# The first pair of feed-forward column tiles turned by VectorE's 32x32 blocks and transfers, in place of TensorE transposes

## What is computed

```
D_MODEL = 1024
SEQ = 256
DEPTH = 2
FFN_HIDDEN = -(-8 * D_MODEL // (3 * 256)) * 256
...
        h = rms_norm(x, norm_ffn[l])
        gate, up = jnp.split(h @ ffn_in[l], 2, axis=-1)
        x = x + (jax.nn.silu(gate) * up) @ ffn_down[l]
```

## Time and profile before

| | |
|---|---|
| median of 3 runs | 904.03 us |
| the profiled execution | 905.12 us |
| its span in the trace | 903.1 us |
| TensorE busy | 893.1 us, 99% of the span |
| VectorE busy | 669.1 us, 74% |
| ScalarE busy | 513.9 us, 57% |
| TensorE's share of the chain that ended last | 93% |

### The profile page before, as it was taken

One profiled execution on the slowest core, in us unless ns is written; L12 is line 12 of the kernel. 1 busy time (PEld: TensorE's weight loads), 2 busy tenths in 40 slices (PEclk: granted clock), 3 DMA queues, 4 the chain that ended last, 5 costly groups with the idle time before them and its releaser, 6 DMA issues.

```text
span 903.1 us, 13837 instructions
## 1 busy us (share of the span) xinstructions
PE 893.1 (99%) x5410; PEld 761.2 (84%) x5410; DVE 669.1 (74%) x1107; ACT 513.9 (57%) x877; POOL 2.4 (0%) x6
## 2 busy tenths in 40 slices
PE   9999999999999999999999999999999999999997
PEld 5999898888887888888889998988888888888885
DVE  6869887778968666656778798767988675665656
ACT  6586556785446544444565866568744554444444
POOL 0000000000000000000000000000000000000000
PEclk9999999999999999999999999999999999999998
DMA  8645646657664777678655374486667467768671
GB/s 294 205 167 164 202 127 180 238 201 230 200 234 153 219 198 251 213 211 261 214 181 175 119 213 155 126 236 229 209 203 237 149 213 221 250 188 259 219 205 46
DMA packets 129056, 180.55 MB, mean 200 GB/s; under 512 B 82272, under 2 KB 88160, under 8 KB 128992
## 3 DMA queue, kind: packets, MB, share of 16 engines
q1 hardware_dynamic: 128560, 179.34, 62.8%
q10 hardware_dynamic: 432, 0.34, 0.1%
HBM read 169.16 MB, written 10.49 MB: 199 GB/s over the span
## 4 chain that ended last, share of the span: by engine, by line
PE 93%; DVE 5%; ACT 1%; issue 0%; ACTq 0%; DVEq 0%
PE bank L620 8%; PE bank L622 7%; PE bank L621 7%; PE bank L492 7%; PE bank L494 7%; PE bank L493 7%; PE bank L697 6%; PE bank L395 5%; PE bank L434 5%; PE bank L436 5%; PE bank L435 5%; PE bank L396 5%; PE bank L397 5%; PE bank L424 2%; PE bank L423 2%; PE bank L422 2%
## 5 line engine op out<-in xcount | busy, mean ns | idle before, releaser
L938 ACT CAST whi<-raw 128x1024 fp32r<-128x1024 f32 x290 | 303.6, 1053 | 296.3 <-PE bank L494 94.5
L1288 DVE TENSOR_TENSOR wlo<-raw,whi 128x1024 fp32r<-128x1024 f32 x290 | 347.6, 1216 | 66.7 <-ACT whi L938 64.1
L395 PE MATMUL bank<-ahi,whi 128*128 128x256 f32 x448 | 129.6, 289 | 0.8 <-DVE tmp L1338 0.8
L396 PE MATMUL bank<-alo,whi 128*128 128x256 f32 x448 | 126.7, 283 | 0.0
L397 PE MATMUL bank<-ahi,wlo 128*128 128x256 f32 x448 | 126.6, 283 | 0.0
L620 PE MATMUL bank<-whi,ahi 128*128 128x512 f32 x288 | 114.8, 399 | 0.6 <-DVE alo L1352 0.5
L622 PE MATMUL bank<-whi,alo 128*128 128x512 f32 x288 | 112.4, 390 | 0.0
L621 PE MATMUL bank<-wlo,ahi 128*128 128x512 f32 x288 | 112.3, 390 | 0.0
L492 PE MATMUL bank<-whi,ahi 128*128 128x512 f32 x288 | 112.2, 390 | 0.0
L494 PE MATMUL bank<-whi,alo 128*128 128x512 f32 x288 | 112.1, 389 | 0.0
L493 PE MATMUL bank<-wlo,ahi 128*128 128x512 f32 x288 | 112.0, 389 | 0.0
(11 more groups left out here) (299 smaller groups left out, 1305.8 us busy)
## 6 DMA issues: line engine op xcount, KB each, us to landing
raw<-stream_dram SPq DMA_DIRECT2D x292, 512.0 KB, 4.7
turned_dram<-proj SPq DMA_DIRECT2D x144, 32.0 KB, 1.7
proj<-turned_dram SPq DMA_DIRECT2D x18, 256.0 KB, 4.6
proj<-gbias_dram SPq DMA_DIRECT2D x12, 256.0 KB, 4.4
probs_dram<-proj SPq DMA_DIRECT2D x8, 192.0 KB, 4.3
proj<-probs_dram SPq DMA_DIRECT2D x2, 768.0 KB, 5.9
par<-params_dram SPq DMA_DIRECT2D x2, 556.5 KB, 6.5
x<-x_dram SPq DMA_DIRECT2D x2, 512.0 KB, 5.3
```

What stands on the lines that cost most here:

```text
L395: pe.matmul(dst, whi_of(m)[:, wcol], hi, start=first, stop=False, skip_group_check=True)
L396: pe.matmul(dst, whi_of(m)[:, wcol], lo, start=False, stop=False, skip_group_check=True)
L938: act.copy(whi_of(m), raw_of(m)).then_inc(*AC.up(("hi", m), "w"))
L1288: dv.tensor_tensor(wlo_of(m), raw_of(m), whi_of(m), ALU.subtract).then_inc(*DV.up(("lo", m), "w"))
```

## The change

Pair 0 takes the second way as well, in both layers. Its transfers stand at SP's f = 8 (writes) and f = 9 (read). `ffn_turned(0)` is 7 in place of 6; the down product stays at f = 8 and 9. The count by which ScalarE knows the returned transfers goes up accordingly. `turn_hidden` is no longer called.

```
         def ffn_turned(j):
 
-            return 6 * j + 6 if j < PAIRS - 1 else 6 * j + 3
+            return 6 * j + 6 if j else 7
...
         def by_transfer(j):
-            return 1 <= j < PAIRS - 1
+            return 0 <= j < PAIRS - 1
...
         def hid_count(l, j):
-            return l * (PAIRS - 2) + j
+            return l * (PAIRS - 1) + j + 1
...
                 for k in range(NH):
                     j, r = divmod(k - 2 * FFN0 - 6, 6)
+                    if k - 2 * FFN0 in (8, 9):
+                        j, r = 0, k - 2 * FFN0 - 8
+                    elif j == 0:
+                        r = None
                     if r == 0 and by_transfer(j):
```

## The result

The changed kernel takes 914.18 us (median of 6 runs, 911.87 to 917.14) against 904.46 (6 runs). The ratio is 1.0109, with a 95% interval of 1.0089 to 1.0128. It is slower by about 9.7 us; 911.6 was forecast, inside a range of 907.4 to 915.4.

What follows compares the result with a forecast made beforehand. TensorE was taken to bound the kernel. To the median of 904.03 us were added 5.6 for net stalls in two layers and 2.0 for one clock fall, giving 911.6 us, range 907.4 to 915.4.

Steps and rivals of the forecast that it cites:

- The bound: Whole kernel: TensorE, busy 99% of the span and 93% of the last chain, sets the time.
- The gain: Before f = 8: removing four transposes a layer saves 0.48 and 0.49 us, 0.97 us in two layers.
- The route: Pair 0's hidden values, from S (start of the first L1799) to the down product: 12.45 us, losing 2.8 a layer.
- The read at 303.90: S + 6.44: SP's queue, priced from pair 1: the read is issued 6.44 us after S, the start of the first L1799.
- the median of 4.6: Pair 0's read: lands 4.6 us after issue, the median of 18 reads ranging from 3.3 to 6.2.
- One fall in two stalls: TensorE's clock behind the stalls at f = 8: drops to half speed once, costing 2.0 us; chance 0.37.
- The two-fall rival: TensorE's clock falls behind both layers' stalls: 913.6 us, up to 915.6 with 3 us each; chance 0.17.
- the bound of 3 us: TensorE after a stall: 6 us of work at half speed lose 3 us, the upper bound for one fall.
- What was priced at nothing: VectorE's block transposes, SP's late loads 93 and 94, work queued behind ScalarE's and VectorE's waits: no cost.
- A quick read: Pair 0's read lands in 2.6 us, taking 2.0 off each layer's 2.8: 905.6 us; chance 0.05.
- A hidden read: Pair 0's read lands within 1.3 us of issue, so 0.97 us are won: 903.1 us; chance 0.04.
- Slower transfers: Writes collide with load 92 or an issue hangs in both layers: 913.0 us, 917 with two falls; chance 0.09.

Runs made afterwards that it cites:

- e8_tanh_first: Changed kernel with pair 0's down product at f = 10 and 11 and pair 1's tanh and hidden values ahead of pair 0's copy and remainder: 904.14 us, ratio 0.9997.
- e9_down12: Changed kernel with pair 0's down product at f = 12 and 13, its copy and remainder at f = 9: 903.53 us, ratio 0.9992.
- e2_load92: Changed kernel with the load of half 92 issued behind pair 0's read instead of before its writes: 914.67 us, ratio 1.0108.
- e3_loads92_93: Changed kernel with the loads of halves 92 and 93 both issued behind pair 0's read: 908.28 us, ratio 1.0045.
- e7_turned6: Changed kernel with pair 0's copy and remainder at f = 6 in place of 7: 914.30 us, ratio 1.0116.
- e1_fill: Changed kernel with unused matmuls filling TensorE's stalls before pair 0's down product, 16 in layer 0 and 10 in layer 1: 911.52 us, ratio 1.0087.
- e4_unused: Changed kernel with pair 0's transfers made but not waited for, TensorE's transposes used as in the kernel before: 904.42 us, ratio 0.9999.
- e5_later: Changed kernel with pair 0's down product two steps later, f = 10 and 11, copy and remainder at f = 8: 904.98 us, ratio 1.0006.

## Why the prediction was right

**The bound.** TensorE sets the end; every us that it stood or ran slowly is in the time: 9.7 by parts, 9.7 between the medians.

**The gain.** Two times 0.48 us were taken from the gap in the stream. The versions with the wait taken away come 0.1 (e8_tanh_first) and 0.7 us (e9_down12) under the kernel before by their medians, which proves nothing at this size. Their traces do: 0.49 us less from S to the end in layer 1, and 0.5 in layer 0, as priced.

**The route.** It was priced at 12.45 us from S. It took 13.65 in layer 0 and 11.94 in layer 1, 12.8 on average, so the two layers lost 4.0 and 2.3 us net in place of 2.8 each, 6.3 against 5.6. The total is near; the terms are not. "The read at 303.90: S + 6.44" was too small for pair 0 by 0.9 and 1.5 us: the collision with load 92, which the prediction left to the range, is real (e2_load92), and an issue hung in layer 0. The landing was quicker than the median of 4.6: 4.2 and 3.1 us. The last term, 1.41, was 1.5. That the errors nearly cancel is partly luck, and partly not: the late writes pushed the reads to 1.9 and 2.0 us behind the load before them, where the 18 stood at 1.2, and reads that far behind a load land sooner (see e3_loads92_93). The prediction took the median "since this read goes out behind a load just as the 18 do"; it did not.

**The clock.** This was the uncertain step. One fall in two stalls at 2.0 us was taken; two came, at 1.7 us each. So the branch that the forecast stood on, one fall (chance 0.37), is not what happened; the one with two falls (0.17) is, and the range held since it reached that far. One fall in two was halfway between two readings of the rows and was read from neither. The mis-sized term is their number, and it is the largest part of what is missing between 911.6 and 914.2. The two-fall rival named 913.6.

The rows for the clock were weak as well: the prediction had 1.9 us into idle time, from the end of the kernel before. In the six stalls that brought a fall (two each in the changed kernel, e2_load92 and e7_turned6) it came 3.2 to 5.1 us after the last matmul had ended, and at the ends of the other ten kernels 2.3 to 4.9 us after. The same holds for the bound of 3 us: the first short weight load stands 6.6 us after the first matmul in the kernel before, but 3.3 to 5.8 us after it in the other ten.

That a fall is what makes the matmuls slow, and that the standing makes the fall, is shown by e1_fill. How often it falls was not to be read from the trace before: stalls of 2.6 us (changed kernel, layer 1), 2.5 (e2_load92, layer 1) and 2.4 (e7_turned6, layer 1) brought a fall, one of 2.4 (e3_loads92_93, layer 0) did not. The Trainium skill, "TensorE: Matmul & The Clock Gate", section "HAM oscillation", says that each wait for a transfer between groups of matmuls can cost a fall, and half of the time spent low: by that rule the changed kernel's two stalls agree, 3.4 us low near each and 1.7 us lost. The two of e3_loads92_93, 2.4 and 1.6 us, brought no fall.

**What was priced at nothing.** The block transposes, the extra transfers, the late loads: e4_unused shows 0.9999. `ffn_turned(0)` = 7: e7_turned6 shows no effect. `hi(92)`, `lo(91)` and pair 1 behind the waiting instructions: no second wait in the changed kernel, as forecast; but only because TensorE had stood still as well. In e5_later, where it had not, just that queue became the next wait, in layer 0. The prediction's sentence "none is late next, as TensorE has stood still as long" was right for the reason it gave.

**The rivals.** A quick read, 2.6 us: the quickest of the 216 reads in all traces took 2.7, and a read of 2.7 in e3_loads92_93 (layer 0) still left a stall of 2.4 us, because it was issued only at S + 7.5. A hidden read: its condition, landing within 1.3 us, was never near. Slower transfers: half true, since the writes did collide with load 92 in both layers and an issue hung in one, but two falls came with it.

**Open.** In layer 0 one of pair 0's eight write issues takes 1.2 to 1.8 us in place of 0.45 in every version that sends pair 0 this way, with and without load 92, except e4_unused. There no issue hangs, but the eighth write lands after 4.0 us, so that the read goes out even later, at S + 8.8. Why was not found. And what decides whether a given stall brings the clock down was not separated from its length.

## What to carry to other kernels

Before an operation is moved from the engine that sets the end to a detour through memory, add up the whole route (engine, issues, landing of the writes, issue of the read, landing, what must still be done) from the same route elsewhere in the trace, and hold it against the steps until the data is wanted: here 12.45 us against the 9.2 that were left (four steps less the 1.7 before S), for a gain of 0.5 a layer. If it doesn't fit, move the consumer; once moved, look at who now stands behind the waiting instruction. And a stall in a stream of matmuls costs its length and often a slow stretch behind it: here 1.7 us on top of 2.8.

## What the runs showed of the hardware that I had not expected

- The 32 KB writes with rows of 128 bytes land in 1.6 to 2.0 us (medians of the 18 groups of the kernel before), and in 2.4 to 2.8 us for pair 0 in the seven kernels that issue load 92 ahead of them, 1.5 us before (14 groups). With load 92 moved behind the read it is 1.6 to 1.8. The time since the last load doesn't decide it alone: the last group of the kernel before has a load 1.4 us ahead of it and a median of 2.0.
- A 256 KB read issued 1.2 us behind a 512 KB load lands in 3.1 to 6.6 us over all eleven traces, one issued 1.8 to 3 us behind in 2.7 to 4.9, and the three with no load in the 3 us before them in 2.7, 2.8 and 3.0. The kernels differ in more than this distance; only e3_loads92_93 was made to change it.
- The clock can fall after work has resumed: 0.8 us into it in layer 0, 1.4 us in layer 1, with 1.00 all through the standing. Both times it stayed low for about 3.4 us of dense matmuls. In e2_load92, where it fell 2.0 us before the stall of layer 0 ended, it was low for about 6.8 us; in e7_turned6, where it fell 0.2 us before that end, for 3.4 again.
